# Three more modulation groups go from TensorE to VectorE, GpSimd and ScalarE

## The reference, cut to what matters

```python
def first_block(x, p, ...):              # gates, recurrence, output projection
    u = _rmsnorm(x, norm_pre)
    y = _rglru_mixer(u, a_w_in, ..., a_w_out)
    h = x + _rmsnorm(y, norm_post)
    return h + sigmoid(h @ ple_w_gate) * (p @ ple_w_proj)

def second_block(x, c, ctx, c_ctx, w_mod, b_mod, ...):
    mod   = silu(c)     @ w_mod + b_mod     # (2048) @ (2048, 12288): 6 vectors of 2048
    sh_m, sc_m, ga_m, sh_f, sc_f, ga_f = split(mod, 6)
    mod_c = silu(c_ctx) @ w_mod + b_mod     # the same matrix, only its first 4096 columns are used
    hc = modulate(rms_norm(ctx, ...), shc_m, scc_m)
    h  = modulate(rms_norm(x, ...), sh_m, sc_m)
    ...
```

## Time and profile before

| | |
|---|---|
| median of 3 runs | 2073.24 us |
| profiled execution, its time | 2074.61 us |
| its span | 2072.8 us |
| PE busy | 2036.8 us (98%) |
| DVE busy | 1526.2 us (74%) |
| ACT busy | 1036.0 us (50%) |
| POOL busy | 56.7 us (3%) |
| bytes read from HBM | 448.35 MB, 218 GB/s over the span |

### The profile page before, as it was taken

How to read it: one execution, slowest core, us unless ns; L and a number is a source line. 1 busy time by engine, 2 the same in 40 slices (tenths; PEclk the granted TensorE clock), 3 DMA queues, 4 the chain that set the end, 5 groups by cost and what they waited for, 6 DMA issues and landing times.

```text
span 2072.8 us, 29839 instructions
## 1 busy us (share of the span) xinstructions
PE 2036.8 (98%) x11900; PEld 1775.6 (86%) x11900; DVE 1526.2 (74%) x2369; ACT 1036.0 (50%) x1548; POOL 56.7 (3%) x57
## 2 busy tenths in 40 slices
PE   8999999999999999999999999999999999999998
PEld 8999999878888888898888888878888888888886
DVE  6888886869798786678888896576766756645655
ACT  6876445656423323545555555555445434434543
POOL 0000010110000000000000000200000000000000
PEclk9999999999999999999999999999999999999999
DMA  7778898667534586444447987555875765565553
GB/s 284 241 255 298 299 340 270 240 198 256 167 101 153 207 297 236 149 136 143 132 143 275 374 300 260 182 165 180 292 263 187 254 212 191 190 213 190 191 192 113
DMA packets 124251, 454.53 MB, mean 219 GB/s; under 512 B 14288, under 2 KB 14672, under 8 KB 123472
## 3 DMA queue, kind: packets, MB, share of 16 engines
q1 hardware_dynamic: 124112, 452.62, 64.4%
HBM read 448.35 MB, written 4.22 MB: 218 GB/s over the span
## 4 chain that ended last, share of the span: by engine, by line
PE 72%; DVE 2%; ACT 1%; issue 0%; DVEq 0%; ACTq 0%
PE bank L923 72%; DVE WL L1643 1%; DVE AR L1650 0%; DVE AR L1643 0%; DVE SR L1650 0%; ACT WH L1228 0%; ACT AR L1228 0%; ACT AR L1229 0%; ACT L1229 0%; PE bank L1080 0%; PE bank L1119 0%; ACT SR L1229 0%; DVE WF L1681 0%; DVE AR L1738 0%; DVE AR L2142 0%
## 5 line engine op out<-in xcount | busy, mean ns | idle before, releaser
L923 PE MATMUL bank<-SR,WH 128*128 128x512 f32 (+1 forms) x5216 | 1395.3, 354 | 16.8 <-DVE WL L1643 7.9
L1643 DVE TENSOR_TENSOR WL<-WF,WH 128x1024 fp32r<-128x1024 f32 x636 | 775.7, 1226 | 266.1 <-ACT WH L1228 262.6
L1228 ACT ACTIVATE WH<-WF 128x1024 fp32r<-128x1024 f32 x636 | 671.5, 1057 | 539.7 <-PE bank L923 472.1
L923 PE MATMUL bank<-SR,WL 128*128 128x256 f32 (+1 forms) x3936 | 924.2, 287 | 1.7 <-DVE SR L1650 1.7
L923 PEld LDWEIGHTS bank<-SR,WH 128*128 128x128 f32 x5216 | 832.2, 190 | 65.9 <-issue 20.5
L923 PEld LDWEIGHTS bank<-SR,WL 128*128 128x128 f32 x3936 | 744.9, 189 | 123.3 <-DVE SR L1650 3.3
L923 PE MATMUL bank<-WH,SR 128*128 128x512 f32 x1280 | 395.0, 389 | 0.0
L923 PEld LDWEIGHTS bank<-WH,SR 128*128 128x128 f32 x1280 | 240.3, 188 | 49.5
L1228 ACT ACTIVATE AR<-bank 128x256 f32<-128x256 f32 (+1 forms) x261 | 110.1, 426 | 291.7 <-PE bank L923 288.0
L923 PE MATMUL bank<-WL,SR 128*128 128x512 f32 x640 | 249.0, 389 | 0.0
L1643 DVE TENSOR_TENSOR AR<-AR 128x256 f32<-128x256 f32 (+3 forms) x374 | 158.3, 455 | 51.8 <-ACT AR L1229 34.8
(11 more groups left out here) (98 smaller groups left out, 563.5 us busy)
## 6 DMA issues: line engine op xcount, KB each, us to landing
WF<-in_mlp SPq DMA_DIRECT2D x256, 512.0 KB, 3.7
WF<-in_mod SPq DMA_DIRECT2D x192, 512.0 KB, 5.3
WF<-in_w_in SPq DMA_DIRECT2D x176, 512.0 KB, 4.5
WF<-in_a_in SPq DMA_DIRECT2D x64, 512.0 KB, 5.4
WF<-in_a_out SPq DMA_DIRECT2D x32, 512.0 KB, 6.4
WF<-in_ple_g SPq DMA_DIRECT2D x32, 512.0 KB, 4.8
WF<-in_w_out SPq DMA_DIRECT2D x32, 512.0 KB, 5.0
WF<-in_pw SPq DMA_DIRECT2D x16, 512.0 KB, 3.7
```

The source lines that it names most:

```text
L923: return tensor.matmul(o, l, r, start=start, stop=stop, skip_group_check=True)
L1228: return scalar.activation(o, x, f, scale=scale)
L1643: return vector.tensor_tensor(o, a, b, op)
```

## The change

Groups 1, 2 and 3 leave TensorE and join 5, 6 and 7 as `EARLY`. Each of the 48 blocks of these six groups is now worked on by three engines. GpSimd multiplies the block by vector "a" into one of two product buffers (4 KB a partition each). ScalarE sums this product by an activation with `accum_out`. VectorE multiplies by vector "b" and sums, once per block where it was twice. VectorE waits for GpSimd (`mul_g`), since its own instruction overwrites the block in `WF`. GpSimd waits for ScalarE's sum of the last but one block (`mod_a`).

The two sums of a block no longer stand where the block becomes ready but at least two weight blocks later, and one weight block apart (`due`). A pair of p blocks now stands at two places each in `xb`, `gate` and `aout`, 6 pairs where there were 18. The v blocks begin in `xb`: the list has 4 in `xb`, 20 in `gate`, 24 in `aout`. The loads of the first vectors and the masks move with them.

```diff
-SUMMED = tuple(range(5, 20)) + (21, 22, 23)
+EARLY = (1, 2, 3, 5, 6, 7)
+SUMMED = EARLY + tuple(range(8, 20)) + (21, 22, 23)
...
-    spread = list(range(32)) + list(range(36, 40))
+    spread = list(range(8)) + list(range(36, 40))
...
+        elif cg < 8:
+            b["nth"] = len(early)
+            early.append(i)
+            steps.append(("modm", i))
+            due.append((max(st["used"] + 2, due[-1][0] + 1 if due else 0), i))
         else:
-            steps.append(("modv", i))
...
+            sum_up(i)
...
+        while due and st["used"] >= due[0][0]:
+            sum_up(due.pop(0)[1])
...
-        add_mod(int(j % 2 or j == 14), 64)
+        add_mod(1 + int(j in (4, 7, 10, 13)), 64)
     for j in range(16):
         add("aout", "a_out", j)
-        if j % 3 == 0:
+        if j in (5, 10):
             add_spread()
-        add_mod(1, 64)
+        add_mod((0, 2, 1, 2, 2, 1, 2, 1, 2, 2, 1, 2, 1, 2, 2, 1)[j], 64)
...
+        def mod_sum(i):
+            b = blocks[i]
+            cg, at = divmod(b["index"], 8)
+            half, x = divmod(at, 4)
+            g = PRODUCTS[b["nth"] % 2]
+            w.wait_ge(mul_g, b["nth"] + 1)
+            scalar.activation(g, g, ACT.Copy, scale=1.0, accum_out=sums(0, half, 4 * cg + x)).then_inc(mod_a, 1)
...
             if cg < 8:
-                halves = f.rearrange("p (a x) -> p a x", x=2 * KB)
-                marked()
-                mark(vector.scalar_tensor_tensor(
-                    UNUSED, halves, 1.0, VEC["a"].rearrange("p (a x) -> p a x", x=2 * KB), ALU.mult, ALU.mult,
-                    accum_out=sums(0, half, 4 * cg + x)))
-                marked()
-                vector.scalar_tensor_tensor(
-                    f, f, 1.0, VEC["b"], ALU.mult, ALU.mult, accum_out=sums(1, half, 4 * cg + x)).then_inc(mod_v, 1)
...
+                w.wait_ge(mul_g, b["nth"] + 1)
+            v = int(cg < 8)
+            vector.scalar_tensor_tensor(
+                f, f, 1.0, VEC["b"], ALU.mult, ALU.mult, accum_out=sums(v, half, 4 * cg + x)).then_inc(mod_v, 1)
...
+        def mod_product(i):
+            b = blocks[i]
+            w.wait_ge(landed[i % NF], 16 * (i // NF + 1))
+            w.wait_ge(s_vec, 16 * USES[b["phase"]][1])
+            if b["nth"] > 1:
+                w.wait_ge(mod_a, b["nth"] - 1)
+            pool.tensor_tensor(PRODUCTS[b["nth"] % 2], WF[:, i % NF, :].rearrange("p (a x) -> p a x", x=2 * KB),
+                               VEC["a"].rearrange("p (a x) -> p a x", x=2 * KB), ALU.mult).then_inc(mul_g, 1)
```

More of the change, by code:

```diff
@@ L127, in timetable @@
             add("xb", "a_in", 2 * j + n)
-            if j > 2 and n:
+            if j in (4, 6) and n:
                 add_spread()
+            add_mod(int(j > 5), 64)
         if j % 2 == 0:
@@ L236, in mod, with sum_up @@
                 st["hold"] = st["used"] + (5 if b["fill"] else 1)
-        else:
-            steps.append(("modv", i))
[L239 to L242, removed]
+        elif cg < 8:
[3 more added lines that the diff above has]
+            due.append((max(st["used"] + 2, due[-1][0] + 1 if due else 0), i))
+        else:
+            sum_up(i)
+    def sum_up(i):
+        b = blocks[i]
+        steps.append(("modv", i))
+        if b["last"] and b["phase"] + 1 < len(PHASES):
+            old, new = USES[b["phase"]], USES[b["phase"] + 1]
+            for n in range(max(old[1], new[0]), new[1]):
+                steps.append(("vector", n, b["n"]))
     def mods_done(lo, hi):
@@ L502, in timetable @@
             begin()
+            assert not due
             for n in range(4):
@@ L662, in build @@
     w_hi, w_lo, prod, mod_v, mod_p = (sem(n) for n in ("w_hi", "w_lo", "prod", "mod_v", "mod_p"))
+    mul_g, mod_a = sem("mul_g"), sem("mod_a")
+    early = sum(b["of"] == "v" and b["index"] < 64 for b in blocks)
     free = [sem(f"free{g}") for g in range(GBANKS)]
@@ L824, in mod_blocks, with sums @@
         return max((b["n"] for b in blocks if b["of"] == "v" and lo <= b["index"] // 8 < hi), default=0)
+    def sums(v, half, n):
+        if half:
+            return SECOND[:, 96 + n:97 + n] if v else SECOND[:, n:n + 1]
+        return (MODC if v else MOD)[:, n:n + 1]
     def piece_of(k):
@@ L1565, in scalar_program @@
                 high(*a)
+            elif what == "modv" and blocks[a[0]]["index"] < 64:
+                mod_sum(a[0])
             elif what == "evac":
@@ L2234, in pool_program, with add_square @@
         pool.memset(ONES[:, :], 1.0).then_inc(ones_ok, 1)
-        for group in range(3):
+        def mod_product(i):
+            b = blocks[i]
+            w.wait_ge(landed[i % NF], 16 * (i // NF + 1))
[4 more added lines that the diff above has]
+                               VEC["a"].rearrange("p (a x) -> p a x", x=2 * KB), ALU.mult).then_inc(mul_g, 1)
+        def add_square(group, ft):
+            w.wait_ge(sq, 16 * group + ft + 1)
+            w.wait_ge(acc, 14 * group + ft - 1)
+            pool.tensor_tensor(ACC, ACC, SQ[ft % 2], ALU.add).then_inc(acc, 1)
+        for what, *a in steps:
+            if what == "modm":
+                mod_product(a[0])
+            elif what == "evac" and a[0][0] == "aout" and 1 <= a[0][1] < 15:
+                add_square(0, a[0][1])
+        for group in range(1, 3):
             for ft in range(1, 15):
-                w.wait_ge(sq, 16 * group + ft + 1)
-                w.wait_ge(acc, 14 * group + ft - 1)
-                pool.tensor_tensor(ACC, ACC, SQ[ft % 2], ALU.add).then_inc(acc, 1)
+                add_square(group, ft)
         w.wait_ge(st_cp, 1)
```

37 lines of the change are left out of this document (18 added, 19 removed).

## The result

The changed kernel took 2183.53 us (median of 4 runs, 2182.96 to 2184.98), the kernel before beside it 2073.31. The ratio is 1.0528, with a 95% interval of 1.0516 to 1.0541: 110 us slower, where 62 were predicted. The profiled execution has a span of 2181.3 us and a time of 2183.23.

A forecast was written before the change was run, and what follows sets the result against it. VectorE, held by GpSimd's products, was to bound the three stretches: 47 us after blocks in hand and early pairs, plus 5 for vectors and 10 for slots; 2073.2 + 62 = 2135 us, range 2100 to 2165.

The forecast's parts named there:

- the prediction's first step: Work leaving TensorE takes 15.5 us off the path, giving 2057.7 us if nothing else moves.
- TensorE's gain: 12 pairs at 1.18 us and three transpose rows at 0.43 us leave TensorE: 15.5 us saved.
- The hold of one product: Each GpSimd product of 1024 elements holds VectorE back 2.12 us; the largest bound was 2.33, the smallest nothing.
- the sum of holds: 48 products hold VectorE 8.5 us at the end of `xb`, 42.4 in `gate`, 50.9 in `aout`.
- VectorE as a bound without gaps: From the end of `xb` through `aout`, VectorE's work bounds the stretches, making them 56.9 us longer than before.
- What VectorE will wait for itself: Idle VectorE adds 5 us for second-phase vectors and 10 for late ring slots at four places in `aout`.
- A stage that looks as if it fits by 1 us: In `gate`, VectorE's own work without holds, 101.7 us, still fits beside TensorE's 102.7.
- Behind `aout`: After the changed stages, from `pleg` on, nothing changes.
- The hold does not grow: Rival, 6%: GpSimd's product lets VectorE's instructions in between, so the 15.5 us come through: 2058 us.
- Ring or hand-over alone: Rival, 4%: without a hold, `aout` loads and waits for products bound the kernel: 2058 + 12 = 2070 us.
- The clock falls with waits: Rival, 8%: TensorE runs at half clock after waits, 36 us on top of 2135: 2171, up to 2200.
- ScalarE's 48 sums: They add 55 us to ScalarE's 152 busy us in the three stretches, hidden in 310 or more.

The follow-up runs named there:

- e9: e5 with the first vectors written and fetched two tiles of `xb` earlier; 2067.92 us.
- e5: The changed kernel with GpSimd filling the product buffer with 1.0 instead of multiplying, and the sums where their block becomes ready, without delay; 2072.1 us.
- e1: The changed kernel with GpSimd filling the product buffer with 1.0, reading nothing, instead of multiplying by vector a; sums still delayed; 2125.91 us.
- e3: The changed kernel with a block's sums where it becomes ready, not two weight blocks or more later; GpSimd's product kept; 2146.79 us.
- e4: The changed kernel's order and delay, but VectorE makes both sums of a block, GpSimd and ScalarE left out; 2152.12 us.
- e6: The changed kernel with both sums of a block on VectorE, where the block becomes ready, without delay; 2100.1 us.
- e8: The kernel before with its sums of groups 5, 6, 7 one weight block later and one weight block apart, nothing else; 2082.79 us.
- e10: e1 with ScalarE's sum moved to where the product is made, VectorE's slot-releasing sum left late; 2144.03 us.

## Why the prediction was wrong

The two causes, each on its own and together:

| us | sums delayed, as changed | sums in place |
|---|---|---|
| reading product on GpSimd | 2183.5 | 2146.8 |
| memset instead | 2125.9 | 2072.1 |
| both sums on VectorE | 2152.1 | 2100.1 |

The account from the 2057.7 us of the prediction's first step to the result: 10.2 that e9 lies above 2057.7, 4.2 for the first vectors (e9 to e5), 36.7 to 53.8 for the delay and 57.6 to 74.7 for the product, 111.4 for these two. 2057.7 + 10.2 + 4.2 + 111.4 = 2183.5. By its stages e9 lost 3.1 us up to the end of `xb` and 7.0 in `gate`, and gained 0.9 in `aout` and 0.6 behind it against the sums below; 1.6 are not of a stage: the profiled execution of before lies 1.4 above the median that the account starts from, and e9's time is 0.2 further from its span.

**TensorE's gain: right as far as shown; its shares by stage: off by a pair.** Before, TensorE ran nine pairs in the window of `gate` and four in that of `aout`, in e5 two in each. So seven pairs left `gate` and two left `aout`, not six and three, and TensorE needs 110.2 - 8.7 = 101.5 us in `gate` and 98.7 - 2.8 = 95.9 in `aout`. In e5 and e9 `aout` takes 95.0. That the predicted 94.7 lies nearer is luck. The whole 15.5 us came in no run: e9, the nearest, took 2067.9 us beside 2074.9.

**The hold of one product: right; the sum of holds: too large by a fifth.** One subtraction was held 2.17 us for 2.12. Over all its instructions VectorE was busy 80.9 us more than in e1, and 81.4 more in e3 than in e5 (1604.8 - 1523.4). That is 1.7 us per product; 101.8 in all had been forecast. The two forms of 1024 elements hold 51.4 (1029.9 - 978.5) and 56.4 of it. Most of the rest lies in forms of 256 elements with two SBUF inputs, while the form with a PSUM source was not held, as the prediction took it. Between 87 and 450 us of the changed kernel:

```profile
L1678 DVE TENSOR_TENSOR SR<-AR,SR 128x256 fp32r<-128x256 f32 x25 | 23.6, 947 | 3.5 <-ACT SR L1252 3.5
...
L1678 DVE TENSOR_TENSOR AR<-bank,AR 128x256 f32<-128x256 f32 x22 | 9.1, 414 | 9.3 <-PE bank L947 9.3
```

In e1 their means are 417 and 418 ns. With VectorE's own waits for products that weren't made (2.7 and 18.2 us more) the product costs VectorE 83.6 and 99.6 us, and the time 57.6 and 74.7. So some 25 us in either pair fell where VectorE would have stood idle anyway; which holds those were is not shown. It is also part of these steps that a memset is shorter than a product (0.95 against 2.79 us).

**VectorE as a bound without gaps: wrong. This is the step that failed.** The section "What VectorE will wait for itself" took 5 us for vectors and 10 for the slots, at four places of `aout` with 2.5 us each. Between 87 us and `plep` VectorE was busy 283 us and the stretch took 357: 74 us idle, where a busy time of 318.6 and 15 of idling were forecast. The 35 us of work too many (23 of holds; 12 of VectorE's own work, 204.4 in e1 for 216.8) hid part of the 59 us of idling too few, so the number came nearer than the mechanism was. The vectors were sized well enough: VectorE stood 6.7 us at the change of phase, until 309.24. The slots were not. The delay alone costs 36.7 us with the product (e3), 53.8 with the memset (e5), 52.0 with both sums on VectorE (e4, e6), and one weight block of delay costs the kernel before 9 us (e8). ScalarE's late sum is not the reason: e4 and e6 have none, and e10 gains nothing by putting it back. What is left is the slot that VectorE's late sum keeps, and SP's queue shows it in each pair of runs: it stood behind v blocks' sums for 264.6 us with the delay and 90.5 without (e3), 213.4 and 40.9 (e1, e5), 242.3 and 100.1 (e4, e6). The error was to look for four bad places in the list. The ring is used in order by one DMA queue, so one slot that comes free late holds back every load behind it, weight blocks and p blocks alike, and SP waited so in 45 places for the 48 blocks. The 0.93 of DMA share in `aout` was a hint: it leaves little room to make up for late loads. No run tests how much of the cost hangs on that share, and none frees the slot early with the sum left late.

**A stage that looks as if it fits by 1 us doesn't.** `gate` needed 101.7 of 102.7 us by the sum of VectorE's work, and with seven pairs gone TensorE leaves it only 101.5. Even without hold and delay it took 108.4. The whole-stage mean hid stretches of 8 to 12 us in which VectorE is full.

**Behind `aout`: wrong by 6 us.** From `plep` to the end of the span it is 1737.6 us, and 1738.1 in e1, against 1731.2 before, 1730.9 in e3 and 1730.8 in e5. It goes with the delay, and it is lost in the first 20 us of `plep`: ScalarE waits 5.0 us for the loads of `in_ple_p` there, and the granted clock is 0.75 between 443.7 and 464. From `pleg` on nothing is lost, as forecast.

**The rivals.** *The hold does not grow* is refuted by the 3.39 us. *Ring or hand-over alone* was priced at 12 us with the same four places; the delay is worth 36.7 to 53.8. *The clock falls with waits*: it did. The granted clock was 0.93, 0.89 and 0.87 in the three stretches, where full speed is 2.4 GHz and the other level 1.2. TensorE was busy 272 us between 87 and 444 for the 242 of e5, and these 31 us are near the 36 that the rival priced. How much of the 110 us is the clock's stays open, since no kernel here had the waits without the lower clock. ScalarE's 48 sums were hidden, as forecast: GpSimd waited 95.4 us for them, but VectorE waited for a product only once, for 6.7 us.

## What to carry to other kernels

Work moved to GpSimd with two SBUF inputs is not free for VectorE: here it cost 1.7 us of its time per product (80.9 over 48), 2.17 in a single case, and the second sum on VectorE itself costs 1.31. e6 against e3 says it in one number, 46.7 us. Before a read of a staged block is put off, ask which slot it keeps and what is queued behind that slot; it is the loads that pay, in another place. A busy mean over a stage can't show that an engine keeps up: look at stretches no longer than the blocks in hand cover, here 8.6 us. And ask the DMA queue itself what it waits for; its 264.6 us behind the late sums name the cause more plainly than the engines' waits do.

## What was new of the hardware

- A memset of 128x1024 fp32 by GpSimd took 0.95 us and lengthened no form of VectorE that shows in a mean (1224 ns for the subtraction, 1226 before); the product with two inputs took 2.35 us at best and held one for 2.17.
- The exclusion works both ways at this length: a product that VectorE's sum preceded took 3.36 us, and then held the subtraction behind that sum.
- VectorE's forms with two SBUF inputs were held at 256 elements too (mean 947 ns for 417 in one of them), the form with one PSUM and one SBUF input was not (414 for 418).
- TensorE's clock fell after a wait of 2 us: in e9 it worked without a gap up to 114.9 us, waited 2.00 us, and from 116.9 to 120.3 a pair of matmuls took 0.63 us where 0.40 is usual. The granted clock was 0.81 over 112 to 120 us; its two levels are 1.2 and 2.4 GHz.
